# Three chained mixer blocks in fp32 on one core: head norms with one root per group, mixer output kept on chip, weight sums on VectorE

## What is computed

```python
# block 2: y_b, y_c
o = o * lax.rsqrt(jnp.mean(o * o, axis=-1, keepdims=True) + NORM_EPS_2)      # over a head of 64
y = merge_heads(o) * gain * jax.nn.silu(gate)
# block 3: q and k of fox, before the attention
q = heads(rmsnorm(q.reshape(B, T, FOX_HEADS, HEAD_DIM), q_norm_w)) ; k likewise
# block 3: output of RWKV-7
mean, var = mean and variance of y over a head
y = ((y - mean) * lax.rsqrt(var + LNX_EPS)) * lnx_w + lnx_b
y = (y + bonus) * g
# block 3: output of fox
o = rmsnorm(o, o_norm_w) * jax.nn.sigmoid(og)
# block 3: x = x + concat(y_rwkv, y_fox) @ w_out ;  x = x + (silu(conv(gate)) * conv(val)) @ w_down
```

## Time and profile before

| what | value |
|---|---|
| median of 3 runs | 5811.05 us (5807.86 to 5812.35) |
| profiled execution, own time | 5812.52 us |
| its span, first to last instruction | 5810.9 us |
| mean granted TensorE clock | 0.921 of full |
| busy: TensorE / VectorE / ScalarE / GpSimd | 84% / 43% / 19% / 15% |
| DMA over the span | 378.61 MB, mean 65 GB/s |

### The profile page before, as it was taken

How to read it: one execution, slowest core, us unless ns; L and a number is a source line. 1 busy time by engine, 2 the same in 40 slices (tenths; PEclk the granted TensorE clock), 3 DMA queues, 4 the chain that set the end, 5 groups by cost and what they waited for, 6 DMA issues and landing times. The chain is left out here.

```text
span 5810.9 us, 44089 instructions
## 1 busy us (share of the span) xinstructions
PE 4890.9 (84%) x16320; PEld 2512.2 (43%) x16320; DVE 2521.5 (43%) x3261; ACT 1119.2 (19%) x1602; POOL 898.6 (15%) x674
## 2 busy tenths in 40 slices
PE   8988677899997988889858597857999728999995
PEld 3434343344443434335523243326888613444442
DVE  4305552634554212225334414554443344755755
ACT  1003231100001003333220101243344321110101
POOL 0014401222221110012011010000000031222220
PEclk9999898999998999889979798978999869999997
DMA  2121202111111221111131013332221121111111
GB/s 99 58 102 34 76 37 91 69 44 44 44 44 62 87 86 39 37 65 63 61 138 43 33 73 115 141 111 65 53 53 48 50 103 66 38 42 43 40 44 69
DMA packets 194463, 378.61 MB, mean 65 GB/s; under 512 B 102919, under 2 KB 104471, under 8 KB 193368
## 3 DMA queue, kind: packets, MB, share of 16 engines
q1 hardware_dynamic: 173320, 315.10, 16.0%
q0 software_dynamic: 12880, 46.14, 2.2%
q10 hardware_dynamic: 8064, 14.68, 0.7%
HBM read 270.84 MB, written 105.02 MB: 65 GB/s over the span
## 5 line engine op out<-in xcount | busy, mean ns | idle before, releaser
L157 PE MATMUL mlp_bank<-mlp_u,mlp_s 128*128 128x512 f32 x864 | 380.9, 597 | 0.0
L889 PE MATMUL first_acc<-first_h,first_w 128*128 128x512 f32 x768 | 332.9, 594 | 0.0
L157 PE MATMUL mlp_bank<-mlp_u,mlp_w 128*128 128x512 f32 x648 | 293.1, 604 | 38.8 <-DVEq L448 38.8
L157 PE MATMUL p_bank<-p_t,p_s 128*128 128x512 f32 x720 | 313.9, 592 | 0.0
L144 POOL TENSOR_TENSOR mlp_s<-mlp_w 128x512 f32<-128x512 f32 (+2 forms) x70 | 90.2, 1288 | 1330.2 <-DMA mlp_w<-in_w_up 749.0
L157 PE MATMUL mlp_bank<-stream_x,mlp_s 128*128 128x512 f32 x608 | 273.3, 592 | 0.0
L157 PE MATMUL mlp_bank<-mlp_x,mlp_s 128*128 128x512 f32 x608 | 273.3, 592 | 0.0
L157 PE MATMUL mlp_bank<-stream_x,mlp_w 128*128 128x512 f32 x608 | 267.1, 592 | 0.0
L157 PEld LDWEIGHTS mlp_bank<-mlp_u,mlp_s 128*128 128x128 f32 x864 | 166.0, 192 | 210.8 <-issue 208.6
L2598 PE MATMUL rwin_half<-in_h,rwin_w 128*128 128x512 f32 x512 | 237.5, 624 | 10.8 <-ACT rwin_half_out L2647 10.8
L215 ACT ACTIVATE mlp_p<-mlp_bank 128x512 f32<-128x512 f32 x70 | 41.4, 591 | 989.6 <-PE mlp_bank L157 989.6
(11 more groups left out here) (621 smaller groups left out, 8460.8 us busy)
## 6 DMA issues: line engine op xcount, KB each, us to landing
mlp_w<-in_w_up SPq DMA_DIRECT2D x76, 512.0 KB, 4.1
proj<-p_ev SPq DMA_DIRECT2D x38, 512.0 KB, 2.7
p_w<-in_w_in SPq DMA_DIRECT2D x36, 512.0 KB, 5.7
mlp_w<-in_w_down SPq DMA_DIRECT2D x32, 512.0 KB, 4.6
first_w<-in_w_in SPq DMA_DIRECT2D x24, 512.0 KB, 3.2
p_w<-in_w_out SPq DMA_DIRECT2D x24, 512.0 KB, 5.7
merge_g<-proj SPq DMA_DIRECT2D x8, 1536.0 KB, 8.1
mlp_w<-in_w_down SPq DMA_DIRECT2D x24, 384.0 KB, 3.5
```

The costliest lines, as they stand in the source:

```text
L157: mm = nc.tensor.matmul(self.bank[product - 1][:, :], lhs[:, p, :], rhs(name, p), start=p == 0, stop=p == kp - 1)
L889: mm = nc.tensor.matmul(acc[m % 2][:, cs], W[m % 2][:, k * P:(k + 1) * P], H[:, k, cs], start=k == 0, stop=k == KD - 1)
```

## The change

Head norms: `head_norm` is replaced by `compact_norm`, which works on groups of four tiles. The squares of a group are summed by a 128x8 selector ("pick") into one 8x1024 PSUM tile (8 heads), so variance, Ln, Exp and Newton run once per group on 8 partitions, and an 8x128 matrix ("back") spreads the root to each tile through PE. Gates are multiplied on GpSimd before the root is known; stores go through SyncE's queue. lnx and fon become one stage, lfn, on a tile Y that the mixers write on chip; no wkv, fox or y3 any more. X is stored to kept2 in n21, dropped before the mixers, and loaded again inside p32. The weight sums move from GpSimd to VectorE: those of the first two jobs ahead of T1 to T4, then those of job n+1 at the start of job n. `products` with `await_last` now runs all seven products on the early pairs before it waits.

```diff
 def sums(self, nc, dve, n, kp):
-        self.await_weights(pool, n)
-        nc.gpsimd.tensor_tensor(s1, a21, a22, ALU.add).then_inc(self.sums_ready, 1)
+        self.await_weights(dve, n)
+        nc.vector.tensor_tensor(s1, a21, a22, ALU.add).then_inc(self.sums_ready, 1)
...
-            some(1, a11, "B11", late).then_inc(self.phases_done, 1)
-            some(2, a12, "B21", late).then_inc(self.phases_done, 1)
-            some(5, s1, "T1", late).then_inc(self.phases_done, 1)
-            some(7, s3, "T3", late).then_inc(self.phases_done, 1)
...
+        if await_last is None:
+            all_seven(range(kp), True, True)
         else:
+            all_seven(range(kp - 1), True, False)
             await_last()
+            all_seven([kp - 1], False, True)
...
@@ mlp
-                for n, job in enumerate(jobs):
-                    f.sums(nc, pool, n, KD // 2 if job[0] == "up" else job[2] // 2)
...
                 dve.wait_ge(gained, KD)
+                for s in range(2):
+                    f.sums(nc, dve, s, KD // 2)
...
                 for n, job in enumerate(jobs):
+                    if n:
+                        add_weights(n + 1)
...
@@ folded_project
-                for n in range(pairs):
-                    f.sums(nc, pool, n, KD // 2)
...
                     for k in range(KD):
                         dve.wait_ge(act_in[k], 16)
+                for s in range(2):
+                    f.sums(nc, dve, s, KD // 2)
...
                 for n in range(pairs):
+                    if 0 < n < pairs - 1:
+                        f.sums(nc, dve, n + 1, KD // 2)
...
@@ compact_norm(nc, name, X, groups, width, heads, pick_in, back_in)
+            @block.sync
+            def _(sp):
+                sp.dma_start(pick[:, :], pick_in).then_inc(picks_in, 16)
+                sp.dma_start(back[:, :], back_in).then_inc(picks_in, 16)
+                for gi, g in enumerate(groups):
+                    for j in range(len(g["tiles"])):
+                        if (gi, j) in x_in:
+                            sp.dma_start(x_of(gi, j), g["src"][j]).then_inc(x_in[gi, j], 16)
...
+                for gi, j in mean_order:
...
+                    both(ring[no % 2], heads[:, :], x_of(gi, j)).then_inc(ring_done, 1)
+                pe.wait_ge(picks_in, 32)
+                for n in range(len(sq_order)):
+                    sums(n)
+                for gi, g in enumerate(groups):
+                    pe.wait_ge(rstd_ready, gi + 1)
+                    for j in range(len(g["tiles"])):
...
+                        both(ring[no % 2], back[:, j * P:(j + 1) * P], root[gi]).then_inc(ring_done, 1)
...
+                    if n >= 4:
+                        act.wait_ge(sq_used, n - 3)
+                    nc.scalar.activation(sq[n % 4][:, :], x_of(gi, j), ACT.Square).then_inc(sq_ready, 1)
+                    if n == ends[gi] and groups[gi]["kind"] in ("sigmoid", "silu"):
+                        for i in range(len(groups[gi]["tiles"])):
+                            act.wait_ge(g_in[gi, i], 16)
+                            nc.scalar.activation(SG[gi, i][:, :], G[gi, i][:, :], ACT.Sigmoid).then_inc(sig_ready, 1)
+                nc.scalar.preload_act_table_set("natural_log_exp_and_others")
+                for gi in range(NG):
+                    roots(gi)
...
+                    if kind in ("silu", "layer"):
+                        ch.step(nc.gpsimd.tensor_tensor(x, x, G[key][:, :], ALU.mult))
+                    if kind != "layer":
+                        pool.wait_ge(sig_ready, gate_order.index(key) + 1)
+                        ch.step(nc.gpsimd.tensor_tensor(x, x, SG[key][:, :], ALU.mult))
...
+                variance(0)
+                n = 0
+                for gi, g in enumerate(groups):
+                    dve.wait_ge(exp_ready, gi + 1)
+                    newton(nc, ch, root[gi][:, :], var[gi][:, :], fix[gi][:, :])
+                    dve.sem_inc(rstd_ready, 1)
+                    if gi + 1 < NG:
+                        variance(gi + 1)
+                    if g["kind"] == "layer":
+                        for j in range(len(g["tiles"])):
...
+                            ch.step(nc.vector.scalar_tensor_tensor(A[gi, j][:, :], A[gi, j][:, :], g["beta"][j], G[gi, j][:, :],
+                                                                   ALU.add, ALU.mult))
+                    for j in range(len(g["tiles"])):
...
+                        ch.step(nc.vector.scalar_tensor_tensor(x, x, scaled_gain[:, n:n + 1], ring[no % 2][:, :],
+                                                               ALU.mult, ALU.mult))
+                        dve.sem_inc(ring_free, 1)
+                        if g["kind"] == "layer":
+                            ch.step(nc.vector.tensor_tensor(x, x, A[gi, j][:, :], ALU.add))
...
@@ rwkv_and_fox
-                        nc.scalar.activation(YO[c % 2][:, :, :], of(job)[:, :, 0:CK], ACT.Copy).then_inc(kept["y"], 1)
+                        nc.scalar.activation(Y[:, 0:NP, c * CK:(c + 1) * CK], of(job)[:, :, 0:CK], ACT.Copy).then_inc(kept["y"], 1)
...
-                        nc.vector.tensor_copy(Y[h // 2 % 2][e, i * P:w], O[e, 0:P]).then_inc(o_kept, 1)
+                        nc.vector.tensor_copy(Y[e, NP + h // 2, i * P:w], O[e, 0:P]).then_inc(o_kept, 1)
...
-            @block.gpsimd
...
@@ build
-                normalise(nc, "n21", M, X, ones, col["ln_g"], EPS2, beta=col["ln_b"])
+                normalise(nc, "n21", M, X, ones, col["ln_g"], EPS2, beta=col["ln_b"], store=tile_rows(kept2))
...
+        with Stage(nc, "tail") as tail:
+            Y = tail.sb("y", [P, KD, T])
...
-                folded_project(nc, "p32", Y, a["w_out3"], KD, dst=M, feed=[tile_rows(y3)[n] for n in range(KD)])
-                scaled_sum(nc, "res3a", M, 1.0, X, store=tile_rows(kept3))
+                folded_project(nc, "p32", Y, a["w_out3"], KD, dst=M, also=(X[:, :, :], rows(kept2)))
+                scaled_sum(nc, "res3a", M, 1.0, X, dst=Y, store=tile_rows(kept3))
+            X = Y
```

More of the change, by code:

```diff
@@ L3461, in build @@
             gate_rows = [1792, 1792 + P, 2560, 2560 + P]
[L3462 to L3465 removed]
+            with Stage(nc, "hgnx") as q:
+                hx = q.sb("x", [P, 4, T])
+                compact_norm(nc, "hgn", [hx[:, j, :] for j in range(4)],
+                             [{"kind": "silu", "tiles": range(4), "src": [heads2[j * P:(j + 1) * P, :] for j in range(4)],
+                               "gate": [proj2[n:n + P, :] for n in gate_rows], "eps": EPS2,
+                               "gain": columns(col["hgrn_g"]) + columns(col["gla_g"]),
+                               "dst": lambda j: [(0, P, y2[256 + j * P:256 + (j + 1) * P, :])]}], HD, heads64, c["pick"], c["back"])
             with Stage(nc, "out2") as q:
@@ L3489, in build, with split_heads @@
-            head_norm(nc, "lnx", lambda j: wkv[j * P:(j + 1) * P, :], lambda j: [(0, P, y3[j * P:(j + 1) * P, :])],
-                      heads64, HD, columns(col["lnx_w"]), 64e-5, centre=True, beta=columns(col["lnx_b"]),
-                      add=lambda j: rw["bonus"][j * P:(j + 1) * P, :], times=lambda j: rw["gate"][j * P:(j + 1) * P, :])
-            head_norm(nc, "fon", lambda j: fox[j * P:(j + 1) * P, :], lambda j: [(0, P, y3[512 + j * P:512 + (j + 1) * P, :])],
-                      heads64, HD, columns(col["fo"]), EPS, gate=lambda j: proj3[f0 + 1536 + j * P:f0 + 1536 + (j + 1) * P, :],
-                      gate_kind="sigmoid")
+            with Stage(nc, "fqkx") as q:
+                hx = q.sb("x", [P, 8, T])
+                def split_heads(to):
+                    return lambda j: [(h * HD, (h + 1) * HD, to[2 * j + h, 0:HD, :]) for h in range(2)]
+                compact_norm(nc, "fqk", [hx[:, j, :] for j in range(8)],
+                             [{"kind": "plain", "tiles": range(4 * i, 4 * i + 4), "scale": (HD ** -0.5, 1.0)[i], "eps": EPS,
+                               "src": [proj3[f0 + j * P:f0 + (j + 1) * P, :] for j in range(4 * i, 4 * i + 4)],
+                               "gain": columns(col[("fq", "fk")[i]]), "dst": split_heads((qa, ka)[i])} for i in range(2)],
+                             HD, heads64, c["pick"], c["back"])
@@ new lines, in build @@
+            fox_forget(nc, proj3[f0 - P:f0 - P + FH, :], a["f_bias"], c["one_rows"], qa, ka)
+        with Stage(nc, "tail") as tail:
+            Y = tail.sb("y", [P, KD, T])
+            rwkv_and_fox(nc, rw, qa, ka, proj3[f0 + 1024:f0 + 1536, :], c["chunk_mask"], c["chunk_wide"], c["causal"], ident, Y)
+            compact_norm(nc, "lfn", [Y[:, j, :] for j in range(8)],
+                         [{"kind": "sigmoid", "tiles": range(4, 8), "eps": EPS, "gain": columns(col["fo"]),
+                           "gate": [proj3[f0 + 1536 + j * P:f0 + 1536 + (j + 1) * P, :] for j in range(4)]},
+                          {"kind": "layer", "tiles": range(4), "eps": 64e-5, "gain": columns(col["lnx_w"]),
```

(2 more changed lines are left out.)

370 lines of the change are left out of this document (175 added, 195 removed).

## The result

| what | before | after |
|---|---|---|
| median, lowest to highest | 5811.6 us (5807.86 to 5812.35) | 5646.34 us (5637.39 to 5653.59) |
| profiled execution, own time and span | 5812.52, 5810.9 us | 5637.39, 5635.7 us |
| mean granted TensorE clock | 0.921 | 0.934 |

The ratio is 0.9716, 95% interval 0.9699 to 0.9733: 2.8% faster. The forecast of 5638 us lies inside the spread of the four runs of after, 8 us under their median.

A forecast was written before the change was run, and what follows sets the result against it. PE, busy 4890.9 of 5810.9 us, was taken as the bound, its waits as winnable. Terms summing to -173.5 took 5812.5 to 5639, the median 1.5 lower: 5638 us, range 5605 to 5690, chance 0.80.

The forecast's parts named there:

- Sum: Whole kernel: fqk -34, hgn -18.4, lfn -91.5, p32 -9.1, starts +6, group ends -29, n21's store +2.5; total -173.5 us.
- Backs at 1.9 us: Head norms: each product spreading the root to a tile takes 1.9 us on PE, 3.8 when cold.
- Picks mostly at 1.9: Head norms: the selector sums mostly take 1.9 us a tile on PE, the full-clock price.
- rival of cold norms: Norms: picks and backs all at half clock, 3.8 us a tile; 5706 us in all, chance 0.07.
- Newton at 3.25 beside GpSimd: hgn: VectorE's Newton steps on 8 partitions take 3.25 us each beside GpSimd's gates; otherwise hgn is 6 us shorter.
- Gap before lfn, p32's start: 1.1 us from the mixers' last copy to lfn; p32's T1 ready 16.7 us after its first fetch, -9.
- Group ends: mlp3: PE's four waits on a group's last pair shrink, to 2.4 us for all but the last; -29 us.
- n21's store +2.5: n21: storing X there adds between 0 and 3.4 us, taken as +2.5.
- Starts +6: Stage starts of mlp1, mlp3, p12, p21, p22, p31: PE waits for VectorE's weight sums and T1, +6 us.
- VectorE drags mlp3: mlp3: costly weight sums on VectorE outlast PE's 48.2 us per two up jobs; 5711 us, chance 0.07.
- group ends unchanged: mlp3: early products wait for banks or sums instead, so group ends gain nothing; 5667 us, chance 0.03.
- slower: Weight waits in VectorE's order delay the quarters that free PE's banks; 2.3 us a set gives 5845, chance 0.03.

The follow-up runs named there:

- e1: The changed kernel run again with nothing altered: 5642.77 us, ratio 0.9720 to the kernel before.
- e8: The kernel before with only the new order of the seven products: 5789.9 us, ratio 0.9968.
- e2: The changed kernel with back products padded by zeros from 8 to 128 rows in all three norms: 5629.4 us, ratio 0.9698.
- e5: The changed kernel with back products zero-padded to 16 rows in hgn, 64 in fqk, 32 in lfn; single run: 5650.57 us.
- e11: The changed kernel with back products zero-padded to 96 rows in hgn, 112 in fqk, 127 in lfn; single run: 5638.03 us.
- e6: The changed kernel with the norms' gate products moved from GpSimd to VectorE: 5640.3 us, ratio 0.9706.
- e7: The kernel before with one slot for every tile of a head norm instead of three: 5757.58 us, ratio 0.9922.
- e10: The changed kernel with weight sums back on GpSimd and the old product order: 5663.88 us, ratio 0.9756.
- e3: The changed kernel with only the weight sums back on GpSimd: 5649.5 us, ratio 0.9735.

## Why the forecast held, and where its steps failed

- **Sum.** Forecast -173.5 against the profiled span. Measured there: -175.2, made of -137.0 in the norm stretches (forecast -153.0), -28.4 from p32's T1 to mlp3's end (forecast -27.5) and -9.8 in all the rest (forecast +7). Against the medians, -165. So the sum was nearer than its parts, by luck: 16 us that the norms fell short by were made up where nothing was forecast to be won. Of the -9.8, `merge` is -7.3 (132.9 us before, 125.6 after) and the stage `rwin` -3.9 (340.2, 336.3), and neither was changed. `merge` takes 134.5 us in e1, and `rwin` 336.6 in e8, which has the old norms. So these two shifts come with the executions that were profiled; no run ties them to the change.
- **Backs at 1.9 us (failed).** "Four backs at PE's pace", "then a cold back 3.8, three more": each ran at 3.5, because the clock never rose, or at 2.9 in fqk's first group, where it fell. fqk was 60.4 instead of 54, hgn 50.7 instead of 47.7, lfn 64.6 instead of 58.5. e2 puts the price back, and with it hgn, fqk and 2.7 of lfn's 6.1 us; the other 3.4 are VectorE's chain, a second term that was sized too small. The forecast took 1.9 since "the rows' forms share the moving columns", and said that "back" had no row; the trace of before held nearer rows that weren't read, products with 64 rows in:

```profile
L2584 PE MATMUL rwin_pa<-rwin_al,rwin_lo 64*128 64x512 f32 x16 | 14.5, 1056 | 0.0
```

```profile
150.94 1.98 PE L916 MATMUL first_ring<-first_fw,first_net 64*128 64x512 f32 x4
...
3759.15 3.65 PE L2584 MATMUL rwin_pw<-rwin_wl,rwin_lo 64*128 64x512 f32 x4 [5.22 <-DMA rwin_lo<-in_loras]
```

  The first is a row of the kernel before, from its groups by line and shape: 1056 ns a record of 512 columns with no idle time before it, where 128-row records of as many columns have 592 ns as their usual length. It warned of the higher price but didn't settle it: the timeline of before has four 64-row records right ahead of such a group that had waited 5.22 us, so the wait could have been the reason, and four others, among 128-row ones in a stretch at clock 1.00, took 1.98 us. Only e2, e5 and e11 separate rows from waits.
- **Picks mostly at 1.9 (held).** 32 records in 13.90 us in lfn, 1.74 a tile, at clock 1.00; 1.9 a tile in fqk and 2.5 in hgn, where they start cold. The rival of cold norms (5706) falls as a whole: it had waits between bursts as its mechanism, and here the clock is high in the picks and low in bursts without a gap. Its price, near 3.8 a tile, came true for the backs alone.
- **Newton at 3.25 beside GpSimd (held).** 2.27, 3.25 and 3.24 us; e6 shows the cause.
- **Gap before lfn, p32's start (held).** 1.1 for 1.1; 17.0 for 16.7, by way of two wrong inputs: the first weights landed 6.2 us after the fetch instead of 5.0, with X's reload on the DMA engines beside them (DMA share 0.95 in that stretch), and the second pair at 11.1 instead of 10.4.
- **Group ends (held; the order is most of it, 22.0 us in e8, and the moved sums the rest).** Forecast -29 and mlp3's start +1.5; measured -28.4, stalls 2.34 us where 2.4 was forecast, and the longest 8.3. The restart is warm: PE's x4 records take 1.98 us behind the stall, against 3.78 before.

```profile
4916.54 1.98 PE L157 MATMUL mlp_bank<-mlp_u,mlp_w 128*128 128x512 f32 x4 [2.34 <-DVEq L458]
```

- **n21's store +2.5 (held).** PE's wait between n21's sums and the sums of the norm behind it grew by 2.5 us. It is 29.88 to 29.93 us in the ten kernels that store X there and 27.34 to 27.37 in the three that don't (before, e7, e8). Before and after:

```profile
3262.67 16.53 PE L592 MATMUL n_total<-n_sq,main_ones 128*128 128x512 f32 x32 [27.35 <-ACT n_sq L605]
...
3246.76 16.97 PE L604 MATMUL n_total<-n_sq,main_ones 128*128 128x512 f32 x32 [29.88 <-ACT n_sq L617]
```

- **Starts +6 (too large).** PE's waits for VectorE at the stages' starts, p32 aside, are 0.41 us in p12, 0.33 in p21 and 0.91 each in mlp1 and mlp3, and none in p22 and p31: 2.6 us. Before had none of them. With p32's 1.50 us, these waits in the projections are (us, times, longest):

```profile
PE p_bank L157 <- DVEq L548: 2.2, 3, 1.5
```

  Up to hgn the kernel is 7.2 us late where 3.4 was forecast. But e10, with GpSimd's sums, is as late (7.3), e8, which is before but for the order, 6.3, e7, unchanged up to there, 3.9, and e3 3.4. So this stretch moves by some 4 us from profile to profile for reasons that the sums don't explain. That stays open.
- **VectorE drags mlp3, group ends unchanged, slower.** None shows: up jobs are without gaps, the waits fell, and no wait for weights holds the banks.

## What to carry to other kernels

- Price a product by rows in, columns moved and the clock it leaves behind: here a string of 16 records with 64 rows or fewer ran at half clock though it had no gap, and padding the operand with zero rows cost less than it gave back. A few such records among full ones did no harm. Look for the nearest row by form before taking one by size.
- Before a stage is rebuilt to shorten its chain, give each tile its own buffer and see what is left: here that alone was 53 of 137 us.
- Work put on GpSimd "beside" VectorE wasn't beside it in these norms: two-input steps on on-chip tiles took turns. Such work belongs where VectorE waits for another engine.

## What the runs showed of the hardware that was not expected

- TensorE's granted clock stayed at 0.50 through 13.0 to 13.9 us of products without a gap where 8, 16, 32 or 64 rows were in use, and even fell so in fqk's first group, which followed picks at full clock (11.79 us for what takes 7.13 warm). It rose with 96, 112, 127 and 128 rows. 8 columns out with 128 rows in don't lower it (lfn's picks, 13.70 us at 1.00). The Trainium skill's "TensorE: Matmul & The Clock Gate" (Part 1, "What's actually happening") ties the clock to how busy PE has recently been; the two groups of e2 and the restarts in `merge` agree, the 8-row products, with PE busy all through, don't, and here the measurement decides. Short runs of 64-row products between 128-row ones leave it at 1.00: four records of L916 in before (1.98 us, clock 1.00 from 150 to 156 us), and those of L2054, which overlap each other (32 records in 2.06 us, then 3.70 us of 128-row ones, and so on; 1.00 from 2680 to 2700 us). How long a run has to be to lower it wasn't tried.
- In one profile each, a 127-row load of 254 KB came 7.29 us later than PE wanted it, while the 128-row one left no wait. The cause is open.
